# Weighing every fourth expert row on VectorE instead of TensorE in a decoder step with a product-key expert layer

## The reference, cut to what matters

```python
q = (xb @ w_query).reshape(PEER_BLOCK, 8, 2, 64)          # 8 heads, two half keys
s = jnp.einsum('thcd,hcnd->thcn', q, keys)                # 128 scores a half
sv, si = lax.top_k(s, 16)
cv, ci = lax.top_k(all 256 sums of the two halves, 16)    # 16 experts a head and token
idx = i1 * 128 + i2
g = softmax(cv)
a = gelu(einsum('thkd,td->thk', expert_u[idx], xb))       # dot with the token's h2
wgt = g * a
y = einsum('thk,thkd->td', wgt, expert_v[idx])            # weighted sum of V rows
```

## Time and profile before

| what | value |
|---|---|
| median of 3 runs | 3940.13 us |
| the profiled execution, its own time | 3936.95 us |
| its span, first to last instruction | 3935.0 us |
| busy: PE, DVE, POOL, ACT | 84%, 64%, 61%, 27% of the span |
| first U gather to last V gather issued | about 631 to 3922 us |
| granted TensorE clock, mean | 0.961 of full speed |
| moved by DMA | 1278.37 MB, of it 1107.43 MB by the gathers |

### The profile page before, as it was taken

The page is one execution under the profiler, slowest core; times in us unless marked ns, Lnnn a source line. Parts: engine busy times, 40 slices in busy tenths (PEclk is TensorE's granted clock), DMA queues, the critical chain, the costliest instruction groups (busy, mean ns, idle before and its releaser), DMA issues.

```text
span 3935.0 us, 36702 instructions
## 1 busy us (share of the span) xinstructions
PE 3292.0 (84%) x10654; PEld 1732.6 (44%) x10654; DVE 2530.8 (64%) x5906; ACT 1077.6 (27%) x2400; POOL 2415.8 (61%) x2146
## 2 busy tenths in 40 slices
PE   3899995987999999999978688778876888789777
PEld 1457773444555565566534233423332334334221
DVE  2355545666787776677646577567756766676663
ACT  1225551222332232243212132123221322222220
POOL 1000002777667776766757777677777777777775
PEclk7999997999999999999989999999999999999999
DMA  6452215999999999999999999999999999999998
GB/s 215 159 175 65 65 54 199 376 378 383 366 349 389 373 388 369 383 343 356 348 398 380 351 371 359 372 365 372 361 371 350 362 363 371 360 368 341 366 365 317
DMA packets 487668, 1278.37 MB, mean 325 GB/s; under 512 B 43592, under 2 KB 189704, under 8 KB 486799
## 3 DMA queue, kind: packets, MB, share of 16 engines
q0 software_dynamic: 304128, 1107.43, 74.9%
q1 hardware_dynamic: 142634, 141.31, 10.8%
q10 hardware_dynamic: 40708, 27.28, 2.2%
HBM read 1247.65 MB, written 30.25 MB: 325 GB/s over the span
## 4 chain that ended last, share of the span: by engine, by line
PE 31%; DMA 24%; POOL 21%; issue 10%; DVE 9%; ACT 5%; SPq 0%; ACTq 0%; DVEq 0%; POOLq 0%
PE bank L1715 18%; DMA v_ring<-in_expert_v_dram,idx 16%; POOL u_ring L650 11%; POOL v_ring L658 10%; PE bank L1549 6%; DMA u_ring<-in_expert_u_dram,idx 5%; PE bank L1690 3%; DMA mod_s<-mod 2%; PE bank L1739 1%; PE bank L1671 1%; DVE prod L1323 1%; ACT sm L744 1%; PE bank L1528 1%; DVE rt L1107 1%; ACT sm L753 1%
## 5 line engine op out<-in xcount | busy, mean ns | idle before, releaser
L1715 PE MATMUL bank<-v_ring,diag 128*128 128x512 f32 (+1 forms) x4224 | 2077.6, 623 | 509.3 <-DMA v_ring<-in_expert_v_dram,idx 404.0
L1323 DVE CUSTOM_DVE_ANT_0 prod<-u_ring,h2b 128x1024 f32<-128x1024 f32 x1056 | 1287.4, 1226 | 907.5 <-DMA u_ring<-in_expert_u_dram,idx 820.7
L650 POOL DMA_INDIRECT u_ring<-in_expert_u_dram,idx x1056 | 1187.9, 1125 | 792.2 <-DVEq L1302 396.1
L658 POOL DMA_INDIRECT v_ring<-in_expert_v_dram,idx x1056 | 1211.7, 1147 | 487.4 <-PE bank L1715 248.5
L1715 PEld LDWEIGHTS bank<-v_ring,diag 128*128 128x128 f32 (+1 forms) x4224 | 758.7, 192 | 1582.4 <-DMA v_ring<-in_expert_v_dram,idx 848.7
L890 ACT ACTIVATE diag<-ident,wgt 128x128 f32<-128x128 f32 x1024 | 357.4, 394 | 665.6 <-PE bank L1715 322.5
L1549 PE MATMUL bank<-hi,whi 128*128 128x512 f32 x832 | 413.5, 497 | 2.4 <-issue 2.4
L1549 PE MATMUL bank<-hi,wlo 128*128 128x512 f32 x832 | 329.1, 396 | 0.0
L1549 PE MATMUL bank<-lo,whi 128*128 128x512 f32 x832 | 328.5, 395 | 0.0
L1101 DVE TENSOR_TENSOR wlo<-wc,whi 128x1024 fp32r<-128x1024 f32 x104 | 127.4, 1225 | 123.4 <-ACT whi L709 117.7
L1549 PEld LDWEIGHTS bank<-hi,whi 128*128 128x128 f32 x832 | 159.1, 191 | 75.7 <-issue 51.1
(11 more groups left out here) (246 smaller groups left out, 2611.5 us busy)
## 6 DMA issues: line engine op xcount, KB each, us to landing
wc<-in_w_in_dram SPq DMA_DIRECT2D x104, 512.0 KB, 6.2
ada_w<-in_w_ada_dram SPq DMA_DIRECT2D x12, 2048.0 KB, 8.1
u_ring<-in_expert_u_dram,idx POOLq DMA_INDIRECT x1056, 6.5
v_ring<-in_expert_v_dram,idx POOLq DMA_INDIRECT x1056, 6.5
wo_sb<-in_w_out_dram SPq DMA_DIRECT2D x2, 4096.0 KB, 20.3
wq_sb<-in_w_query_dram SPq DMA_DIRECT2D x2, 4096.0 KB, 28.5
q_st<-q_dh ACTq DMA_DIRECT2D x65, 64.0 KB, 5.5
xt<-in_x_prompt_dram SPq DMA_DIRECT2D x8, 512.0 KB, 4.7
```

The source lines that it names most:

```text
L650: pool.indirect_dma_start(out=u_ring[k % RING][:, :], out_offset=None, in_=eu, in_offset=bass.IndirectOffsetOnAxis(ap=idx[n % IDXS][:, k:k ...
L658: pool.indirect_dma_start(out=v_ring[k % RING][:, :], out_offset=None, in_=ev, in_offset=bass.IndirectOffsetOnAxis(ap=idx[n % IDXS][:, k:k ...
L1323: V.tensor_tensor_reduce(out=prod[k % 2][:, :], in0=u_ring[k % RING][:, :], in1=h2b[t % 2][:, :], scale=1.0, scalar=0.0, op0=ALU.mult, op1 ...
L1715: last = M(banks(c, 1)[0:parts, :], diag[k % DIAGS][:, 0:parts], v_ring[k % RING][:, c * 512:(c + 1) * 512], start=first, stop=final)
```

## The change

A row (n, k) with n below 64 and k % 4 == 2 is weighed by DVE. There are 4 such rows in each of 64 units, 256 in all. DVE multiplies it by its column of `wgt` and adds it to `y_sum`, a tile of SBUF that takes the place of the two `prod` buffers. The other 800 rows stay with PE. The dot's product is written over the U row that it reads, and the dot's wait for an earlier dot is gone. The order of POOL's gathers is as before; its wait for a V buffer is for DVE's count where DVE read that buffer last. `finish_y` of a prompt tile has one more instruction, since the PSUM sum and `y_sum` are first added.

```diff
+def on_dve(n, k):
+    return n < NT * PH and k % RING == 2
...
-        prod = row(["prod0", "prod1"], 11264, D)
+        y_sum = place("y_sum", 11264, D)
...
             def gather_v(n, k):
                 at = n * TOPK + k
                 if at >= RING:
-                    pool.wait_ge(rows_done, at - RING + 1)
+                    if on_dve((at - RING) // TOPK, (at - RING) % TOPK):
+                        pool.wait_ge(rows_added, dve_rows(at - RING))
+                    else:
+                        pool.wait_ge(rows_done, pe_rows(at - RING))
...
                 for k in range(TOPK):
-                    make_diag(n - 1, k)
+                    if not on_dve(n - 1, k):
+                        make_diag(n - 1, k)
...
             def dot_rows(n, k):
-                if at >= 2:
-                    w(dots_done, at - 1)
...
-                V.tensor_tensor_reduce(out=prod[k % 2][:, :], in0=u_ring[k % RING][:, :],
+                V.tensor_tensor_reduce(out=u_ring[k % RING][:, :], in0=u_ring[k % RING][:, :],
...
+            def add_row(n, k):
+                at = n * TOPK + k
+                w(v_in[k % RING], 16 * (at // RING + 1))
+                if dve_rows(at) % (PH * TOPK // RING) == 1:
+                    ins = V.tensor_scalar(y_sum[:, :], v_ring[k % RING][:, :], wgt[n % 2][:, k:k + 1], None, ALU.mult)
+                else:
+                    ins = V.scalar_tensor_tensor(out=y_sum[:, :], in0=v_ring[k % RING][:, :], scalar=wgt[n % 2][:, k:k + 1],
+                                                 in1=y_sum[:, :], op0=ALU.mult, op1=ALU.add)
+                ins.then_inc(rows_added, 1)
...
             def finish_y(t):
-                w(rows_done, min((t + 1) * PH, UNITS) * TOPK)
+                w(rows_done, pe_rows(min((t + 1) * PH, UNITS) * TOPK - 1))
...
+                if t < NT:
+                    w(rows_added, (t + 1) * PH * TOPK // RING)
+                    link(V.tensor_tensor(y[:, :], banks(0, 2), y_sum[:, :], ALU.add))
+                    dve.sem_inc(y_read, 1)
+                    link(V.tensor_tensor(y[:, :], y[:, :], G2[:, :], ALU.mult))
...
                 for k in range(TOPK):
                     dot_rows(n, k)
+                    if n and k and on_dve(n - 1, k - 1):
+                        w(rows_added, dve_rows((n - 1) * TOPK + k - 1) - 1)
+                        add_row(n - 1, k - 1)
...
             def add_row(n, k):          # TensorE
+                if on_dve(n, k):
+                    return
...
-                w(diag_made, at + 1)
+                w(diag_made, pe_rows(at))
```

More of the change, by code:

```diff
@@ L61, with pe_rows, dve_rows @@
 S_BASE = 854
+def on_dve(n, k):
+    return n < NT * PH and k % RING == 2
+def pe_rows(at):
+    return sum(not on_dve(i // TOPK, i % TOPK) for i in range(at + 1))
+def dve_rows(at):
+    return at + 1 - pe_rows(at)
 def proj_slot(b):
@@ L350, in build @@
         q_in = [sem(f"q_in_{r}") for r in range(2)]
-        dots_done, rows_done, s_ps, s_out, best_made, gate_exp, idx_made, gelu_made, wgt_made, diag_made = (
-            sem(n) for n in ("dots_done", "rows_done", "s_in_psum", "s_out", "best_made", "gate_exp",
+        dots_done, rows_done, rows_added, s_ps, s_out, best_made, gate_exp, idx_made, gelu_made, wgt_made, diag_made = (
+            sem(n) for n in ("dots_done", "rows_done", "rows_added", "s_in_psum", "s_out", "best_made", "gate_exp",
                              "idx_made", "gelu_made", "wgt_made", "diag_made"))
@@ L886, in make_diag @@
                 at = n * TOPK + k
-                if at >= DIAGS:
-                    w(rows_done, at - DIAGS + 1)
+                if at >= DIAGS and not on_dve((at - DIAGS) // TOPK, k % DIAGS):
+                    w(rows_done, pe_rows(at - DIAGS))
                 base, parts = (ident, P) if n < NT * PH else (sel_s, NS)
@@ L1311, in weigh @@
                 if n >= 2:
-                    w(rows_done, (n - 1) * TOPK)
+                    w(rows_done, pe_rows((n - 1) * TOPK - 1))
                 link(V.tensor_tensor(wgt[n % 2][:, :], act_dot[n % 2][:, :], gate[n % 2][:, :], ALU.mult))
@@ L1460, in finish_y @@
                 parts, y = P if t < NT else NS, h2b[t % 2]
-                w(rows_done, min((t + 1) * PH, UNITS) * TOPK)
+                w(rows_done, pe_rows(min((t + 1) * PH, UNITS) * TOPK - 1))
                 if t in (0, NT):
                     w(e_g2_in, 16 if t == 0 else 32)
-                link(V.tensor_tensor(y[0:parts, :], banks(0, 2)[0:parts, :], G2[0:parts, :], ALU.mult))
-                dve.sem_inc(y_read, 1)
+                if t < NT:
[3 more added lines that the diff above has]
+                    link(V.tensor_tensor(y[:, :], y[:, :], G2[:, :], ALU.mult))
+                else:
+                    link(V.tensor_tensor(y[0:parts, :], banks(0, 2)[0:parts, :], G2[0:parts, :], ALU.mult))
+                    dve.sem_inc(y_read, 1)
                 w(x2_in, t * 16 + 16)
```

## The result

The changed kernel took 3978.93 us, the median of 6 runs (3965.28 to 3983.80); before took 3932.14 us over its 6 runs. The ratio over all these runs, by their means (3976.8 and 3935.7), is 1.0105, 95% interval 1.0076 to 1.0133: slower by 1.05%, some 41 us, where 1.2% was forecast. (The two medians alone would give 1.2%.) The profiled execution, 3965.28 us, is the fastest of the six and stands 28 us above the profiled one of before, so the traces show part of the loss only.

The account below looks back on a forecast made before the run. DMA engines and POOL were taken to bound nearly half the time, PE the projection from 1200 to 1980 us. Terms -20 + 38 + 15 + 10 + 3 = +46 gave 3983, stated as 3986 us (+1.2%), range 3905 to 4060.

Parts of the forecast that it names:

- the prediction's own signs of being wrong: Gathers' means stay, the stretch after 2160 us is no longer, or that before 1980 shrinks by over 40 us.
- PE's relief, -20: 256 rows leaving PE save 20 us from 1200 to 1980 us, where PE sets the pace; bounds 0 and 37.
- Gathers held by the adds, +38: POOL's gathers starting under two-input adds lose 0.27 us an add in the paced stretches: +38 us; bounds 0 and 61.
- Adds held by gathers: Each of the 256 DVE adds might be held by a gather: up to 120 us named, nothing in the sum.
- V gathers behind adds, +15: V gathers wait for late adds, one in four of 153 by 0.4 us: +15 us; bounds 0 and 76.
- finish_y, +10: One more 1.22 us instruction and a hand-over at the end of 8 tiles: +10 us; bounds 0 and 12.
- The projection's first 200 us, +3: From 1000 to 1200 us PE gains and DVE, 185 of 200 us busy, loses: +3 us; bounds -5 and +15.
- The product in place, 0: Writing the dot's product over the U row and removing the dot's wait changes nothing.
- DVE's idle time of 907.5 us before dots: DVE's idle time before dots, said to cover any extra 0.06 us a dot from writing in place.
- A (PE's relief worth more): PE's late rows release V buffers late in 1000 to 1980 us; relief gives -37 us, 3903 us; chance 0.19.
- B (it cancels): Relief of 20 to 37 us against finish_y's 10 and a low POOL cost: 3935 to 3960 us; chance 0.20.
- Rival C: The wait for the add becomes the bound, half of 256 adds late by 1 us: 4080 us; chance 0.13.

Follow-up runs that it names:

- e4_left_out: The changed kernel with the 256 moved rows gathered but left out of the sum, no add on VectorE: ratio 0.9985 to the kernel before.
- e10_five_five: All rows with TensorE, product in place, freed buffers making U and V rings of five each: ratio 0.9839 to the kernel before, 3860.74 us.
- e3_both: All rows with TensorE, product in place, an unused two-input VectorE instruction at each of the 256 places: ratio 1.0127 to the kernel before.
- e6_add_first: The changed kernel with each add ahead of dot (n, k) instead of behind it: ratio 1.0143 to the kernel before.
- e2_five: The changed kernel with a fifth V buffer, for VectorE's rows, in the second prod buffer's place: ratio 1.0019 to the kernel before.
- e12_late_tiles: The changed kernel with rows moved only in tiles 4 to 7 (128 rows): ratio 1.0038 to the kernel before.
- e8_both_one_input: All rows with TensorE, an unused one-input VectorE reduction at each of the 256 places, nobody waiting for it: ratio 1.0080 to the kernel before.

## Why the prediction was right, and where its steps were not

The side, the size (+1.2% against +1.05%) and the range were right. POOL and the DMA engines as the pace, and PE's work as mostly covered, were the readings that gave the side. The way the size was reached was not right, and two of the prediction's own signs of being wrong came: the gathers' means did not both rise, and the stretch after 2160 us is 3 us behind, within what one trace can be off another, where nearly 50 were forecast. The terms:

- **PE's relief, -20.** Measured -6 (e4_left_out), inside its bounds. The reason given, that the DMA engines stood at their limit with a share of 1.00, holds only in part: e10_five_five runs 379 GB/s and 627 gathers in 1000 to 1980 us, at a share of 1.01, where before had 367 and 611 at 0.99. More was to be had there, by buffers and with PE busy for 98% of the stretch.
- **Gathers held by the adds, +38.** This step failed. In the changed kernel no add held a gather, and the gathers take 12 us less than before. The prediction let the add start when the 0.08 us read of the accumulator ends, and put that end 0.08 us behind the dot's; by its own row the read ends with the dot, and the add starts with the read. So the next gather comes 0.09 us before the add ends, which costs it nothing (last section). Gathers held by a second input do exist where the timing differs: 32 us in e3_both, 74 in e6_add_first.
- **Adds held by gathers: up to 120 us of DVE time named, 0 in the sum.** 201 of the 248 adds began while a gather ran, and took 1.275 to 1.284 us, their usual time. The zero was right.
- **V gathers behind adds, +15.** The wait is there, 121 us in 83 waits, far more than 15, but it stands in the place of 113 us of waiting for PE, which the prediction counted apart. What it costs net can't be separated from the buffer's worth: e2_five gives 0.86%, and so does a buffer with no rows moved.
- **finish_y, +10.** 17 us with some 8 to either side for each of the two kernels compared.
- **The projection's first 200 us, +3,** and with it the place of the loss. The forecast put 53 us, more than its net 46, into 700 to 900 and after 2160 us; the profile after has 22 of 28 before 1980 us, where reciprocals of 3.35 us stand between dots. e12_late_tiles agrees: half the rows, moved where the forecast had all of the loss, cost 0.38%.
- **The product in place, 0.** Right.

What no term had: one more instruction on VectorE's queue costs time though no gather waits for it and it holds none. e8_both_one_input prices that at 0.80%. The prediction took it as covered by DVE's idle time of 907.5 us before dots. That idle time was no cover: 820.7 us of it was waiting for U rows, whose gathers wait in turn for the dots, and a fifth U buffer, beside a fifth V buffer, is worth 0.73%.

That the size came out is luck. The +38 was not there, and costs that the sum lacked stood in its place. It would be as easy to be content with another sum: 0.80% for the instruction, 0.42% for finish_y, -0.15% for the relief make 1.07%, beside 1.05% measured. But each has 0.2% to either side, the same sum with e3_both's 1.27% gives 1.54%, and the 0.80% is paid in gathers held by dots 0, 4, 8 and 12, which the change doesn't show (97.2 us against 97.5); its profile shows waits for late adds instead. What is shown is that the instruction on VectorE costs about as much as the whole loss, with rows moved or without, and that TensorE's relief gives almost nothing back.

The bounds add up to 3898 and 4104 us, not 3903 and 4095; the range stated is inside both.

Of the rivals, A (PE's relief worth more) is out by e4_left_out and B (it cancels) by the interval. Rival C named the right wait and overrated its net cost.

Still open: where the rest of the loss goes that the profiled executions don't show (14 of 31 us in e8_both_one_input, 11 of 41 in the change), and what share of it the late V release has by itself.

## What to carry to other kernels

Idle time before an instruction is only slack if nothing in a ring waits for that instruction; follow the buffer once around (issue, landing, reader, release, issue) before calling an engine's idle time free. When a loop's pace is such a round trip, moving work from a busy engine to a less busy one can buy nothing if the new reader is in the same ring, and the SBUF that a change frees may be worth more as a buffer than the change. A forecast that lands by cancelling terms should be checked term by term before its reasons are used again.

## What the runs showed of the hardware

When a dot holds a gather, the gather ends 0.81 us after the dot. In the 14 traces, 12297 gathers began at least 0.06 us into a dot: each took 0.937 us, or the time to the dot's end plus 0.811 us if that is longer, within 0.006 us for 99% of them. So a gather that begins in the dot's last 0.13 us loses nothing, and one that begins near its front up to 1.05 us. Of the 349 that began in a dot's first 0.04 us only 4 were held. The other way round nothing is held: the 10711 dots that began while a gather ran took 1.26 us at most.

What an added instruction costs therefore depends on where the next gather falls, and 0.06 us of the instruction's length can decide it. The first fence is from the timeline of after, the second from that of e3_both:

```profile
2239.41 1.23 DVE L1339 CUSTOM_DVE_ANT_0 u_ring<-u_ring,h2b 128x1024 f32<-128x1024 f32 x1 [2.00 <-DMA u_ring<-in_expert_u_dram,idx]
2239.76 1.69 POOL L664 DMA_INDIRECT u_ring<-in_expert_u_dram,idx  x1 [0.31 <-issue]
...
2240.56 1.28 DVE L1350 SCALAR_TENSOR_TENSOR y_sum<-v_ring,wgt,y_sum 128x1024 f32<-128x1024 f32 x1
...
2241.75 0.93 POOL L675 DMA_INDIRECT v_ring<-in_expert_v_dram,idx  x1 [0.30 <-issue]
```
```profile
2267.96 1.27 POOL L664 DMA_INDIRECT u_ring<-in_expert_u_dram,idx  x1 [0.30 <-issue]
2268.34 0.08 DVE L1339 DVE_READ_ACCUMULATOR2_ANT dot<- 128x1 f32 x1
2268.34 1.22 DVE L1344 SCALAR_TENSOR_TENSOR y_sum<-h2b 128x1024 f32<-128x1024 f32 x1
2269.48 1.22 DVE L1339 CUSTOM_DVE_ANT_0 u_ring<-u_ring,h2b 128x1024 f32<-128x1024 f32 x1
2269.53 1.98 POOL L675 DMA_INDIRECT v_ring<-in_expert_v_dram,idx  x1 [0.30 <-issue]
```

In both a gather is held by a dot and ends 0.89 us after the dot's accumulator read began; the next starts 0.30 us later. After, it falls into the last 0.1 us of a 1.28 us add and takes its 0.93 us. In e3_both the idle instruction is 1.22 us long, the next dot starts 1.14 us behind its start, and the gather, 0.05 us into that dot, takes 1.98. After a hold POOL and VectorE run in step, so a price of "so much a held gather" made from random starts doesn't carry over to an instruction that stands behind another.

The Trainium skill (SBUF — State Buffer, "Who interferes with whom") has the contention of two SBUF inputs with a GpSimd read for the instruction's whole length; the 1.98 us agrees for a gather that starts inside it, and the 0.93 us shows that the last 0.1 us costs a gather nothing. That a gather which starts first holds the dot, the 10711 dots do not bear out.

A second thing without a price: PE's mean granted clock fell from 0.961 to 0.901 (0.97 to 0.87 from 2160 to 3800 us), and a row's matmul went from 623 to 686 ns in the mean. It follows how many rows PE weighs: 0.900 to 0.903 in the profiled execution of every kernel where it leaves out one in four, 0.926 in e12_late_tiles, 0.960 to 0.966 where it weighs all. In e4_left_out the clock is 0.903 too and the time still 0.9985.
